# A packed norm, six more slabs by seven products, centred values and fewer bank waits in a two-block kernel

## The reference, cut to what matters

```python
# first block, behind the RWKV scan; wkv is a linear function of v in each head
mean = jnp.mean(wkv, axis=-1, keepdims=True)
var = jnp.mean(jnp.square(wkv - mean), axis=-1, keepdims=True)
y = ((wkv - mean) * lax.rsqrt(var + GN_EPS)).reshape(B, S, RWKV_WIDTH) * ln_w + ln_b
bonus = jnp.sum(rh * kh * r_k, axis=-1, keepdims=True) * vh

# second block, each layer: h @ w_in gives dq, dk (1024 columns each), dv, cq, ckv, kr, gl
a = jax.nn.softmax(s, axis=-1)
w = a[:, :, 0] - lam * a[:, :, 1]
o = jnp.concatenate(outs, axis=1)                     # 8 heads of 128
o = _rmsnorm(o, subln_g) * (1.0 - lam_init)
g = jax.nn.sigmoid(gl + b_gate)
m = g_a * (o_a @ w_branch_diff) + g_b * (o_b @ w_branch_mla)
```

## Time and profile before

| what | value |
|---|---|
| time, median of 3 | 2604.66 us (2604.38 to 2609.56) |
| the profiled execution's own time | 2605.08 us |
| its span, first to last instruction | 2603.1 us |
| mean granted clock of TensorE | 0.993 |
| PE / PEld / DVE / ACT / POOL busy | 97 / 82 / 39 / 14 / 5 % |
| mean DMA | 233 GB/s, 607.72 MB in all |

### The profile page before, as it was taken

The page is one execution under the profiler, slowest core; times in us unless marked ns, Lnnn a source line. Parts: engine busy times, 40 slices in busy tenths (PEclk is TensorE's granted clock), DMA queues, the critical chain, the costliest instruction groups (busy, mean ns, idle before and its releaser), DMA issues.

```text
span 2603.1 us, 74060 instructions
## 1 busy us (share of the span) xinstructions
PE 2518.7 (97%) x33806; PEld 2146.4 (82%) x33806; DVE 1002.7 (39%) x1856; ACT 365.6 (14%) x842; POOL 130.6 (5%) x114
## 2 busy tenths in 40 slices
PE   8999999999999999999999999999999999999998
PEld 8966778887698577876994778769999998999997
DVE  5663464633477734444666235440000001000002
ACT  1001241210100023401000234120000001000000
POOL 0000000000100001400000014010000000000000
PEclk9999999999999999999999999999999999999999
DMA  6445242013444542345435323579999999999996
GB/s 260 148 144 196 105 146 110 4 59 130 146 170 150 194 166 82 130 166 209 164 114 197 140 104 129 232 259 368 426 427 426 426 426 401 426 427 426 426 425 256
DMA packets 58054, 607.72 MB, mean 233 GB/s; under 512 B 7365, under 2 KB 7493, under 8 KB 12353
## 3 DMA queue, kind: packets, MB, share of 16 engines
q1 hardware_dynamic: 52272, 587.74, 56.7%
q0 software_dynamic: 5648, 18.04, 2.1%
HBM read 599.66 MB, written 6.09 MB: 233 GB/s over the span
## 4 chain that ended last, share of the span: by engine, by line
PE 90%; DVE 4%; DMA 3%; ACT 2%; issue 1%; SPq 0%; DVEq 0%; ACTq 0%
PE bank L2804 19%; PE bank L314 16%; PE bank L470 16%; PE bank L2817 10%; PE bank L497 7%; PE bank L324 5%; PE bank L1676 3%; PE bank L1798 3%; DMA slot<-in_experts 3%; PE bank L1244 2%; PE bank L1662 1%; DVE arena L2517 1%; PE bank L972 1%; PE bank L2736 1%; PE bank L1267 1%
## 5 line engine op out<-in xcount | busy, mean ns | idle before, releaser
L2804 PE MATMUL bank<-arena,slot 128*64 128x84 f32 x14336 | 540.9, 236 | 12.9 <-issue 7.3
L2804 PEld LDWEIGHTS bank<-arena,slot 128*64 128x64 f32 x14336 | 527.4, 137 | 19.2 <-issue 17.2
L314 PE MATMUL bank<-h_cm,slot 128*128 128x256 f32 x1472 | 324.1, 381 | 0.4 <-ACT h_cm L361 0.2
L314 PEld LDWEIGHTS bank<-h_cm,slot 128*128 128x128 f32 x1472 | 280.1, 191 | 44.4 <-issue 6.5
L3003 DVE TENSOR_TENSOR ff<-ff,bank 128x168 f32<-128x168 f32 x112 | 36.9, 330 | 638.8 <-PE bank L2804 634.6
L2817 PE MATMUL bank<-ff,arena 128*64 128x84 f32 x5376 | 212.8, 238 | 7.6 <-issue 7.2
L2817 PEld LDWEIGHTS bank<-ff,arena 128*64 128x64 f32 x5376 | 202.0, 138 | 13.4 <-issue 13.4
L470 PE MATMUL bank<-arena 128*128 128x128 f32 x1584 | 187.8, 275 | 1.1 <-DVE arena L560 1.1
L470 PEld LDWEIGHTS bank<-arena 128*128 128x128 f32 x1584 | 182.2, 192 | 1.3 <-DVE arena L560 1.3
L314 PE MATMUL bank<-arena,slot 128*128 128x256 f32 x608 | 133.3, 380 | 2.3 <-DVE arena L2520 2.3
L470 PEld LDWEIGHTS bank<-h_cm,slot 128*128 128x128 f32 x1056 | 123.1, 195 | 10.2 <-issue 10.2
(11 more groups left out here) (474 smaller groups left out, 2899.6 us busy)
## 6 DMA issues: line engine op xcount, KB each, us to landing
slot<-in_experts SPq DMA_DIRECT2D x112, 2048.0 KB, 16.1
arena<-in_experts SPq DMA_DIRECT2D x84, 1024.0 KB, 11.8
slot<-in_ffn SPq DMA_DIRECT2D x22, 2048.0 KB, 8.3
x_tm<-in_experts SPq DMA_DIRECT2D x28, 1024.0 KB, 11.6
slot<-in_ffn SPq DMA_DIRECT2D x22, 1024.0 KB, 4.9
slot<-in_dense SPq DMA_DIRECT2D x11, 2048.0 KB, 7.8
slot<-in_dqk SPq DMA_DIRECT2D x8, 2048.0 KB, 7.7
slot<-in_g SPq DMA_DIRECT2D x8, 2048.0 KB, 7.7
```

What stands on the lines that cost most here:

```text
L314: ins = pe.matmul(ps[0:m, j * S:(j + 1) * S], w[:, k * width + c0:k * width + c0 + m], rhs[:, k, :], start=k == 0, stop=k == ks - 1)
L2804: ins = pe.matmul(bank[64 * c:64 * c + 64, m * PLACES:(m + 1) * PLACES], weights[:, c0:c0 + 64], CURRENT[:, k, :], start=k == 0, stop=k == ...
```

## The change

The change has four parts.

1. **Bank waits.** PE's program keeps, bank by bank, the highest count that it has waited for, and leaves out a wait for a count no higher than that, in `fill` and wherever PE called `drained`. Some waits of later heads on the same copies are left out by hand.
2. **Centred values.** The mean over a head of the scan's output is linear in the values. DVE now subtracts each head's mean from V_TM, a pair of groups at a time: at the start for the first pair, then at the end of every second turn of the loop for the next one. PE waits for it before it reads V_TM (`values_centred`). The output in K has mean zero then, the matmuls `gnm` and DVE's subtraction (line 1615) are gone, and ACT squares K.
3. **Query-key slabs.** In both layers of the second block slabs 1, 2 and 3 of `dqk` are done by seven products as well, with sums by POOL in a slot of their own and sums of products by DVE; ACT's two copies of each are gone.
4. **Packed norm.** The sums of squares go to 32 rows for each pair of heads, four matmuls side by side in one bank (`dn`); ACT's root and DVE's reciprocal work on 128x512, the reciprocal also carries 1 - lam_init, and four matmuls (`dnb`, as `head_spread`, line 723) spread it to 128 rows, out of which DVE multiplies output and gain in one operation for each bank. On ACT `g2(0)` moves behind MLA's first softmax and the squares, `g2(1)` behind its second, and the root stands before MLA output 1. On DVE one bank of gate sums, not two, stands between the MLA maximum and the row scaling.

```diff
+        SEVEN_SLABS = [("dqk_", 1), ("dqk_", 2), ("dqk_", 3)] + [("g2_", n) for n in range(4)]
...
-                if name == "g2_":
-                    stream.append(((f"g2sum_{l}", n), None, 0))
+                if (name, n) in SEVEN_SLABS:
+                    stream.append(((f"sum_{name}{l}", n), None, 0))
...
+        def pe_bank_free(pe, bank, count):
+
+            if count > pe_knows_free[bank]:
+                pe.wait_ge(psum_free[bank], count)
+                pe_knows_free[bank] = count
...
-            if turns[bank]:
-                pe.wait_ge(psum_free[bank], turns[bank])
+            pe_bank_free(pe, bank, turns[bank])
...
+        def pe_drained(pe, key):
+
+            pe_bank_free(pe, *job[key][0:2])
...
                 for p in range(2):
-                    drained(pe, ("LM", j, a, p))
+                    pe_drained(pe, ("LM", j, a, p))
+                pe.wait_ge(named("values_centred"), j + 1)
...
-            pe.wait_ge(named("wkv_ready"), 1)
-            for b in range(4):
-                ps = fill(pe, ("gnm", b), next_bank())
-                filled(pe.matmul(ps[:, :], headones, K[:, 2 * b:2 * b + 2, :], start=True, stop=True), ("gnm", b))
             pe.wait_ge(named("centred_squared"), 4)
...
+            act.wait_ge(named("wkv_ready"), 1)
             for b in range(4):
-                drained(act, ("gnm", b))
-                act.activation(CUM[:, 2 * b:2 * b + 2, :], TMP[:, 2 * b:2 * b + 2, :], ACT.Square
+                act.activation(CUM[:, 2 * b:2 * b + 2, :], K[:, 2 * b:2 * b + 2, :], ACT.Square
...
+            def centre_values(j):
+                t, k0 = PAIRS[j]
+                heads = V_TM[:, t, k0 * P:(k0 + 4) * P].rearrange("p (h d) -> p h d", d=HD)
+                ch.step(nc.vector.tensor_reduce(stat[:, 32:40], heads, AX, ALU.add))
+                nc.vector.scalar_tensor_tensor(heads, spread(stat[:, 32:40], HD), -1.0 / HD, heads, ALU.mult, ALU.add
+                                               ).then_inc(named("values_centred"), 1)
...
             key_products(first, 1)
+            centre_values(0)
             level_zero(first)
...
                 mask_level(*new, 4)
+                if new[1] and new[0] + 1 < len(PAIRS):
+                    centre_values(new[0] + 1)
...
-            for n in range(4):
-                weights = first_load[f"g2_{l}", n]
-                load, w = gate_sums(l, n)
+            for name, n in SEVEN_SLABS:
+                weights = first_load[f"{name}{l}", n]
+                load, w = slab_sums(l, name, n)
...
+        def slab_tiles(name, n):
+
+            if name == "g2_":
+                return gates2[:, 4 * n:4 * n + 4, :].rearrange("p (g m) s -> p g m s", g=2)
+            return arena[:, 0:4096].rearrange("p (g k s) -> p g k s", g=2, s=S)[:, :, 2 * n:2 * n + 2, :]
...
             def dqk(a):
+                if a:
+                    pe_slab_seven(pe, l, "dqk_", a, SEVEN)
+                    return
...
             def diff_scores(a):
-                for m in range(2):
-                    drained(pe, ("dqk", l, a, m))
+                for key in [("dqk_", l, a, b) for b in (2, 3)] if a else [("dqk", l, 0, m) for m in range(2)]:
+                    pe_drained(pe, key)
...
-            pe.wait_ge(named("oa_stages"), 4 * l + 1)
+            pe.wait_ge(named("oa_stages"), 5 * l + 1)
+            ps = fill(pe, ("dn", l), next_bank())
             for b in range(4):
-                ps = fill(pe, ("dn", l, b), next_bank())
-                filled(pe.matmul(ps[:, :], ones, QD[:, 2 * b:2 * b + 2, :], start=True, stop=True), ("dn", l, b))
+                ins = pe.matmul(ps[32 * b:32 * b + 32, :], ones[:, 0:32], QD[:, 2 * b:2 * b + 2, :], start=True, stop=True)
+            filled(ins, ("dn", l))
             mla_turn(1)
-            pe_gate_seven(pe, l, 3, SEVEN[0:4])
+            pe_slab_seven(pe, l, "g2_", 3, SEVEN[0:4])
             mla_out(1)
-            pe_gate_seven(pe, l, 3, SEVEN[4:7])
+            pe_slab_seven(pe, l, "g2_", 3, SEVEN[4:7])
+            pe.wait_ge(named("oa_stages"), 5 * l + 4)
+            for b in range(4):
+                head_spread(pe, ("dnb", l, b), b, OA_INVERSE)
...
-            g2(0)
             diff_out(3)
             act_softmax(act, l, "mla", 0, 12 * l + 8)
             for a in range(4):
                 drained(act, ("do", l, a))
             act.activation(QD, OA, ACT.Square).then_inc(named("oa_stages"), 1)
-            g2(1)
+            g2(0)
             mla_out(0)
             act_softmax(act, l, "mla", 1, 12 * l + 10)
+            g2(1)
+            act.wait_ge(named("oa_stages"), 5 * l + 2)
+            act.activation(OA_INVERSE, OA_INVERSE, ACT.Sqrt).then_inc(named("oa_stages"), 1)
+            mla_out(1)
             g2(2)
-            mla_out(1)
-            act.wait_ge(named("oa_stages"), 4 * l + 2)
-            act.activation(QD, QD, ACT.Sqrt).then_inc(named("oa_stages"), 1)
             g2(3)
...
             latent_norm()
+            dqk(1)
             diff_turned(0)
             diff_weights(1)
+            dqk(2)
             diff_turned(1)
             diff_weights(2)
             rotate()
+            dqk(3)
             diff_turned(2)
...
-            mla_weights(0, lambda: gate(1, 0, 1))
-            gate(1, 2, 3)
+            mla_weights(0, lambda: gate(1, 0))
+            gate(1, 1, 2, 3)
...
-            gate(3, 0, 1)
-            dve.wait_ge(named("oa_stages"), 4 * l + 3)
-            ch.step(v.reciprocal(QD, QD))
-            init = 0.8 - 0.6 * math.exp(-0.3 * l)
-            ch.step(v.tensor_tensor(OA, OA, QD, ALU.mult))
-            v.tensor_scalar(OA, OA, col(f"subln{l}"), 1.0 - init, ALU.mult, ALU.mult).then_inc(named("oa_stages"), 1)
-            gate(3, 2, 3)
+            dve.wait_ge(named("oa_stages"), 5 * l + 3)
+            v.reciprocal(OA_INVERSE, OA_INVERSE).then_inc(named("oa_stages"), 1)
+            gate(3, 0, 1, 2, 3)
+            for b in range(4):
+                ps = full(dve, ("dnb", l, b))
+                part = OA[:, 2 * b:2 * b + 2, :]
+                ins = v.scalar_tensor_tensor(part, ps[:, :].rearrange("p (k s) -> p k s", s=S), col(f"subln{l}"), part,
+                                             ALU.mult, ALU.mult)
+                free(ins, ("dnb", l, b))
```

More of the change, by code:

```diff
@@ L1238, in pe_rwkv_chunks @@
                     for half in range(2):
-                        drained(pe, ("tm", name, t, half))
+                        pe_drained(pe, ("tm", name, t, half))
             def by_chunk(ps, a, width, c0, left, right):
@@ L1612, in dve_rwkv_chunks @@
             dve.sem_inc(named("wkv_ready"), 1)
-            for b in range(4):
-                ps = full(dve, ("gnm", b))
-                ins = nc.vector.scalar_tensor_tensor(TMP[:, 2 * b:2 * b + 2, :], ps[:, :].rearrange("p (k s) -> p k s", s=S),
-                                                     -1.0 / HD, K[:, 2 * b:2 * b + 2, :], ALU.mult, ALU.add)
-                free(ins, ("gnm", b))
             ps = full(dve, ("gnv", 0))
@@ L1622, in dve_rwkv_chunks @@
             for b in range(4):
-                drained(dve, ("gnm", b))
-            for b in range(4):
                 ps = full(dve, ("gnb", b))
@@ L1772, in pool_gate_sums, with slab_product, pe_slab_seven @@
                 add(w[2], quarter_w(s, 0, 0), quarter_w(s, 1, 0), ALU.subtract).then_inc(done, 4)
-        def gate_product(q):
+        def slab_product(q):
             r = SEVEN.index(q)
             return r // 2, slice((r % 2) * S, (r % 2 + 1) * S)
-        def pe_gate_seven(pe, l, n, products):
-            weights = first_load[f"g2_{l}", n]
-            load, w = gate_sums(l, n)
+        def pe_slab_seven(pe, l, name, n, products):
+            weights = first_load[f"{name}{l}", n]
+            load, w = slab_sums(l, name, n)
             s = weights % SLOTS
@@ L1787, in pe_gate_seven @@
             for q in products:
-                b, c = gate_product(q)
-                key = ("g2", l, n, b)
+                b, c = slab_product(q)
+                key = (name, l, n, b)
                 ps = fill(pe, key, next_bank()) if c.start == 0 else PS[job[key][0]]
-                if n == 0 and q == 6:
+                if (name, n) == SEVEN_SLABS[0] and q == 6:
                     pe.wait_ge(named("x_quarters"), 4 * l + 4)
@@ L2093, in pool_extras @@
         def pool_extras(pool, l):
-            pool.wait_ge(named("oa_stages"), 4 * l + 1)
+            pool.wait_ge(named("oa_stages"), 5 * l + 1)
             pool.dma_start(PLE_TM, dram["ple"][l]).then_inc(named("ple_loaded"), 16)
@@ L2155, in diff_out @@
                 for b in range(2):
-                    drained(pe, ("dt", l, a, b))
-                for t in range(T):
-                    drained(pe, ("dv", l, a // 2, t))
+                    pe_drained(pe, ("dt", l, a, b))
+                if a % 2 == 0:
+                    for t in range(T):
+                        pe_drained(pe, ("dv", l, a // 2, t))
                 ps = fill(pe, ("do", l, a), next_bank())
```

(54 more changed lines are left out.)

74 lines of the change are left out of this document (39 added, 35 removed).

## The result

The changed kernel takes 2583.19 us, the median of six runs (2579.22 to 2586.81), against 2604.32 before (now of six runs as well); the ratio is 0.9916 (0.9903 to 0.9928). The prediction said 2583.5, between 2576 and 2594. The profiled execution took 2584.06 us with a span of 2582.0, 21.1 less than before.

A forecast was written before the change was run, and what follows sets the result against it. PE, busy 97% of the span, was taken as the bound, level with weight loads at the experts. 7.2 + 2.6 + 9.3 + 2.0 + 0.5, less 0.3, gave 21.3 us off 2605.08; 0.4 off for the median: 2583.5, range 2576 to 2594.

The forecast's parts named there:

- Slabs: Second block's six query-key slabs: 1.1 to 1.3 us gained in each by seven products, 7.2 us taken.
- The copies: ACT's copies in query-key slabs, replaced by DVE's sums: only the last sum is late, cost 0 to 0.1 us.
- Packed norm: Differential norm in the second block: four matmuls side by side plus a spread gain 1.3 us a layer, 2.6 in all.
- Waits: Second block's mixers: PE's waits for L2320, L2327, L2481 and L2520 all go, 9.3 us with both layers.
- Centred values: Scan and group norm: 2.9 us gained at the norm, 0.9 paid for DVE's centring, net 2.0.
- the gain of 2.9: Group norm: 5.19 us before the sums of squares replaced by 2.3 us of ACT's squares.
- Repeated waits: Scan's groups and mixers: leaving out satisfied waits gains 0.5 us, at most 6, at least 0.
- The lock: Rival, second block: POOL's sums block DVE's operations on SBUF, 8 us lost in two layers, 2591.5 us; chance 0.10.
- the 1 us allowed: Sign at the experts: their length stays unchanged within 1 us.
- the terms that the prediction names for the lower end of its range: Lower end, 2576 us: repeated waits at 0.03 us each, and 7.8 us gained for the slabs.

The follow-up runs named there:

- e3: The kernel before with the six query-key slabs by seven products and nothing else: 2626.17 us, ratio 1.0078.
- e1: The kernel before with TensorE's repeated bank waits left out and nothing else: 2860.18 us, ratio 1.098.
- e4: The kernel before with the packed norm and the new orders on ACT and DVE, plain query-key slabs: 2616.38 us, ratio 1.0041.
- f3: The changed kernel with ACT's g2(0) and g2(1) and DVE's gate banks where they were before: 2590.79 us.
- h2: The changed kernel with two matmuls of no use on TensorE behind the last state sum, while ACT squares: 2581.76 us, ratio 0.9904.
- g1: The changed kernel with the group norm's four squares shared, two by ACT and two by DVE: 2582.29 us, ratio 0.9913.
- h3: The changed kernel with squares shared by ACT and DVE, nine useless matmuls in each of six turns, 42 waits at the start: 2596.89 us, ratio 0.9969.

## Why the prediction was right

- **Slabs:** 7.2 us forecast; 6 x (13.81 - 12.50) = 7.9 measured. The copies were put at 0 to 0.1 and are a gain: the gap of 0.07 us behind each turn is gone and the scores take 1.51 for 1.58, 0.4 us a layer. In e3 it is gone too, in e1 and e4 not, so it belongs to DVE's sums in place of ACT's copies.
- **Packed norm:** 2.6 forecast; 3.44 - 0.99 - 1.07 is 1.4 a layer, and MLA turn 1 behind it takes 1.46 for 1.31: 2.5.
- **Waits:** 9.3 forecast, all gone. f3 shows that the orders do it for ACT's two; the one for L2520 stands in e3 (2.3) and is gone in e4 with the packed norm; the one for DVE's row scaling is gone in e3, e4 and f3, so no single part is shown to remove it. Slabs alone (7.3 us in both mixers) and norm with orders alone (12.4) make 19.7 of the 21.5 measured together. Most of the last 2 is the lower clock behind the wait that the slabs alone lengthen, 13.81 us for 12.51 in layer 0; the orders remove that wait.
- **Centred values:** net 2.0 forecast, 1.0 measured. The start cost 0.44 (0.55 forecast) and the other three centrings nothing: from the first values to the states it is 121.3 us before and after. The sums of squares came as forecast, 2.3 us behind DVE's last addition to the states. The step that failed is the gain of 2.9, which took the clock behind the squares as unchanged: some 1.5 of it (0.87 and 0.61) went back to the clock. The matmuls removed had kept TensorE busy in that gap, and h2, with two of no use in it, gets the 1.5 back.
- **Repeated waits:** 0.5 forecast, 0 measured. e1 reaches the first unit 0.7 us later than the kernel before. Stood in a row with nothing to hide them, such instructions are 0.05 us each (5.4 / 104).
- **The lock:** the row showed one block, and the prediction worked out four for a whole set of sums, 9.4 us. With a whole set of sums beside them eight scalings took 10.8 us for 2.4, 8.4 more, some four operations of POOL's 2.4. So the trace agrees with one block for each POOL operation. In layer 0 DVE was done at 1042.75 and PE wanted them at 1044.35: 1.6 us were spare (the prediction had put the end near 1050 and the need at 1047.5), and the rival stayed a rival by that little.
- **The ends:** 1.0 us is lost between layer 1's mixer and the first unit, and 1.7 at the experts (0.5 in the second profile), more than the 1 us allowed. In the first of these TensorE's products behind the norm (L2587 and L336) take 10.7 us for 8.9 before, in both profiles, with the clock at 0.68 for 0.81. The gather of the token rows ends last there in the first profile and not in the second. Why the clock is lower there isn't shown.

The total fits better than its parts, and that is luck: 2.7 us more than forecast in the second block's mixers and 1.3 of chance at 224 us stand against 1.5 less for centred values and repeated waits and 2.7 lost at the ends. Nor do the terms that the prediction names for the lower end of its range make 2576: 2583.5 - 5.5 - 0.6 is 2577.4.

Right by the sum, then, and also by something that it left out. The experts were taken as a stage that only inherits its start. That they lose 22 to 250 us by where a loop falls in the instruction stream was in no term and in no rival; the change adds 592 instructions in matmuls and their weight loads, all parts together, takes away 93 waits, and ends 13 short of a whole number of blocks. With the waits kept, a part that I priced at nothing, it ends 95 past one, and the same prediction would have been wrong by 32 us.

## What to carry to other kernels

Ahead of a loop with a long body count the instructions that an edit adds or removes on its engine, and read the instruction queue's packets in the page first: where they grow, no part's time can be read from the total, only stage by stage. Put a wait that is worth nothing down as instructions, not as time. And when matmuls are taken out of a gap on TensorE, ask what the clock does behind it.

## What the runs showed of the hardware

- The place of TensorE's loops: 8 blocks fetched in the experts at 13 short to 0, nine more at each of three returns of the outer loop at 34 to 95 further (22 to 32 us), and nine every 80 us or so at 104 short (253 us). Where exactly the bounds lie was not measured.
- A TensorE gap of 3.0 us was followed by a granted clock of 0.50 in six of six profiles; one of 2.2 us, in g1 and in h3, was not. Of four waits of 2.3 us in the second block three were followed by 0.57 to 0.66 (f3 in both layers, e3 in layer 0) and one by 1.00 (e3 in layer 1), so no length that decides can be read from these runs.
- POOL's sums and DVE's scalings in SBUF: 10.8 us for 2.4, one block for each POOL operation.
